# RWKV scan of a four-layer decoder step: the turned keys come out of the score products, and of the samples' state update only two row sums stay in the scan, the new state being formed during the output projection

## The reference, cut to what matters

```python
def step(S, inp):
    r_t, w_t, k_t, v_t, kk_t, a_t = inp
    sa = jnp.einsum('bhvk,bhk->bhv', S, -kk_t)
    S = (S * w_t[:, :, None, :] + sa[..., None] * (kk_t * a_t)[:, :, None, :]
         + v_t[..., None] * k_t[:, :, None, :])
    return S, jnp.einsum('bhvk,bhk->bhv', S, r_t)
...
y = y * lnx_w.astype(jnp.float32) + lnx_b.astype(jnp.float32)
bonus = jnp.sum(rh * kh * r_k.astype(jnp.float32), axis=-1, keepdims=True) * vh
out = ((y + bonus.reshape(B, T, D)).astype(x.dtype) * g) @ w_o
```

## Time and profile before

| what | value |
|---|---|
| median of 3 runs | 3062.38 us (3061.74 to 3062.84) |
| the profiled execution | 3060.58 us, its span 3058.5 us |
| busy: PE, DVE, ACT, POOL | 2906.5, 1550.4, 1050.5, 1327.6 us |
| the scan's loops, 927 to 1135 us | PE busy 187.25 of 208 us, DVE 160.74 |
| `out` of layer 1 | about 1204.9 to 1253.5 us |

### The profile page before, as it was taken

The page is one execution under the profiler, slowest core; times in us unless marked ns, Lnnn a source line. Parts: engine busy times, 40 slices in busy tenths (PEclk is TensorE's granted clock), DMA queues, the critical chain, the costliest instruction groups (busy, mean ns, idle before and its releaser), DMA issues.

```text
span 3058.5 us, 75513 instructions
## 1 busy us (share of the span) xinstructions
PE 2906.5 (95%) x30897; PEld 2751.0 (90%) x30897; DVE 1550.4 (51%) x2142; ACT 1050.5 (34%) x2027; POOL 1327.6 (43%) x949
## 2 busy tenths in 40 slices
PE   6999999998988989899999999989999999899998
PEld 6998999988977876899998799879999899799998
DVE  3435666127257775566612162466660345566612
ACT  4224333225443332433322443343332322433322
POOL 3443444442435554344444263534444344344443
PEclk8999999999999999999999899999999999899999
DMA  7544333543320003433354322443335543133332
GB/s 269 166 157 150 95 91 96 160 152 114 105 56 4 4 4 84 162 91 90 91 169 137 102 77 85 161 149 91 90 102 157 163 128 91 59 91 90 94 92 84
DMA packets 465628, 332.72 MB, mean 109 GB/s; under 512 B 19915, under 2 KB 435609, under 8 KB 465123
## 3 DMA queue, kind: packets, MB, share of 16 engines
q1 hardware_dynamic: 461400, 325.24, 34.4%
q10 hardware_dynamic: 4010, 4.22, 0.6%
HBM read 319.62 MB, written 10.20 MB: 108 GB/s over the span
## 4 chain that ended last, share of the span: by engine, by line
PE 56%; issue 5%; DVE 4%; POOL 3%; ACT 2%; DMA 1%; SPq 0%; POOLq 0%; DVEq 0%; ACTq 0%
PE banks L1616 33%; PE banks L1624 16%; POOL ct L894 2%; PE banks L2075 1%; DVE h L2557 1%; PE banks L1922 1%; PE banks L1577 1%; DVE proj L2501 1%; PE banks L1639 1%; PE banks L1710 0%; DMA s_state<-in_state_wkv_b_dram 0%; ACT conv L1065 0%; DVE proj_b L2501 0%; POOL mmt L885 0%; DMA w_raw<-in_ffn_w_up_dram 0%
## 5 line engine op out<-in xcount | busy, mean ns | idle before, releaser
L766 POOL TENSOR_TENSOR w_lo<-w_raw,w_hi 128x1024 fp32r<-128x1024 f32 x395 | 1005.2, 2545 | 1113.2 <-ACT w_hi L966 1093.2
L1616 PE MATMUL banks<-u_hi,w_hi 128*128 128x260 f32 x4064 | 835.5, 287 | 13.7 <-ACT w_hi L966 8.8
L1616 PE MATMUL banks<-u_lo,w_hi 128*128 128x260 f32 x4064 | 826.4, 285 | 0.0
L1616 PEld LDWEIGHTS banks<-u_hi,w_hi 128*128 128x128 f32 x4064 | 628.5, 190 | 27.1 <-issue 15.2
L1616 PEld LDWEIGHTS banks<-u_lo,w_hi 128*128 128x128 f32 x4064 | 631.1, 190 | 1.6
L966 ACT ACTIVATE w_hi<-w_raw 128x1024 fp32r<-128x1024 f32 x402 | 424.4, 1056 | 454.4 <-PE banks L1624 293.0
L1624 PE MATMUL banks<-u_hi,w_lo 128*128 128x260 f32 x4064 | 527.7, 282 | 0.0
L1624 PEld LDWEIGHTS banks<-u_hi,w_lo 128*128 128x128 f32 x4064 | 502.2, 187 | 1.5
L1616 PE MATMUL banks<-hid_hi,w_hi 128*128 128x260 f32 x1664 | 336.3, 283 | 0.0
L1616 PE MATMUL banks<-hid_lo,w_hi 128*128 128x260 f32 x1664 | 335.2, 283 | 0.0
L2991 DVE TENSOR_TENSOR csb<-proj 128x520 f32 (+1 forms) x42 | 29.9, 712 | 471.1 <-ACT proj L1033 471.1
(11 more groups left out here) (463 smaller groups left out, 3925.0 us busy)
## 6 DMA issues: line engine op xcount, KB each, us to landing
w_raw<-in_ffn_w_up_dram SPq DMA_DIRECT2D x176, 512.0 KB, 3.6
ada_raw<-in_ada_w_dram SPq DMA_DIRECT2D x96, 512.0 KB, 4.7
w_raw<-in_ffn_w_down_dram SPq DMA_DIRECT2D x64, 448.0 KB, 3.6
w_raw<-in_sconv_w_in_dram SPq DMA_DIRECT2D x48, 512.0 KB, 4.9
ada_ahead<-in_ada_w_dram SPq DMA_DIRECT2D x36, 512.0 KB, 7.3
ada_ahead_down<-in_ada_w_dram SPq DMA_DIRECT2D x36, 512.0 KB, 6.5
w_raw<-in_ffn_w_down_dram SPq DMA_DIRECT2D x32, 512.0 KB, 3.7
ada_pro<-in_ada_w_dram SPq DMA_DIRECT2D x6, 2048.0 KB, 20.5
```

Source lines behind the costliest of these rows:

```text
L766: pool.tensor_tensor(w_lo[:, s, :, :], w_raw[:, s, :, :], w_hi[:, s, :, :].bitcast(F32), ALU.subtract).then_inc(lo_done, 1)
L1616: pe.matmul(tile_ps[slot][half][0:width, 0:HALF], w_hi[:, s, k, 0:width], x[:, k0 + k, half * HALF:(half + 1) * HALF], start=start and k = ...
```

## The change

1. **Turned keys from the score products.** The moving operand `ZR` gets the identity as a third block of 64 columns, so the same product that makes the scores with B (or K) also leaves B (or K) turned. `turn_keys` is gone. `tok` exists twice, and ACT copies the turned keys per pair (`keys_out`, 128x128) behind the `t1` copies of levels 1 to 4, and the values before `uu`.
2. **Samples: two row sums in the scan.** `sample_rows` keeps four instructions per chunk (two products, two row sums, both from the old state). The output row follows from them and two dot products (`key_dots`).
3. **Samples: the new state in `out`.** `decay_state(c)`, five linked instructions of 128x512 for each eighth, 40 in all, runs on VectorE between the tile squares. SP's store of `s_state` moves behind the loads of `out` and ahead of those of `up`, and waits for `s_y_done` 2.

```diff
+                    def thirds(o, j):
+                        return o[:, HD:7 * HD].rearrange("p (n two t) -> p n two t", two=2, t=HD)[:, :, j, :]
...
-                        both(lambda rs: o[rs, HD:3 * HD], lambda rs: b["B"][rs, i, :], lambda rs: b["ZR"][rs, i, :])
+                        both(lambda rs: thirds(o, 0)[rs], lambda rs: b["B"][rs, i, :], lambda rs: b["ZR"][rs, i, :])
...
-                        both(lambda rs: o[rs, 3 * HD:5 * HD], lambda rs: b["K"][rs, i, :],
+                        both(lambda rs: thirds(o, 1)[rs], lambda rs: b["K"][rs, i, :],
...
                         if one_more:
                             pe.wait_ge(scores_masked, 4 * w + 8)
+                            pe.wait_ge(tok_ready, 6 * w + 10)
                             turn_values(cn, qn)
...
-                            pe.wait_ge(keys_built, w + 2)
-                            turn_keys(qn)
                             turn_inverse(w + 1, qn)
...
+                    def keys_out(w, q, i):
+                        act.wait_ge(scores_masked, 4 * w + i + 1)
+                        act.activation(tok[q][:, i, 0:2 * HD], bank[4 + (i + 1) % 4][:, SCW:SCW + 2 * HD], ACT.Copy)\
+                           .then_inc(tok_ready, 1)
...
+                            if one_more and lvl:
+                                keys_out(w + 1, 1 - q, lvl - 1)
...
+                        if one_more:
+                            values_out(w + 1, 1 - q)
                         act.wait_ge(u_mm, w + 1)
...
-                        if one_more:
-                            act.wait_ge(st_mm, w + 1)
-                            tokens_out(w + 1)
...
-                                sample_state(c, 5 * q)
-                            if lvl == 3 and q == 0:
-                                sample_state(c, 1)
-                        for j in range(2):
-                            sample_state(c, 4 * q + 2 + j)
+                                sample_rows(c, 2 * q)
+                        sample_rows(c, 2 * q + 1)
...
-                        sample_state(c, 4 * q + 4)
...
                     dve.wait_ge(sstate_loaded, 32)
-                    b0, s0, PER = base[0], step[0], 2 * 2 + 9
+                    for i, row in enumerate((4, 1)):
+                        link(dve.tensor_tensor(s_tmp[:, 0, :], s_vec[:, row, :], s_vec[:, 0, :], ALU.mult))
+                        link(dve.tensor_reduce(key_dots[:, i:i + 1], s_tmp[:, 0, :], AX.X, ALU.add))
+                    link(dve.tensor_tensor(s_vec[:, 0, :], s_vec[:, 0, :], s_vec[:, 5, :], ALU.mult))
+                    b0, s0, PER = base[0], step[0], 2 * 2 + 4
...
+                    def decay_state(c):
+
+                        vs, W = slice(KT * c, KT * (c + 1)), s_part[:, :, :]
+                        S = s_state[:, vs, :]
...
+                        link(dve.tensor_tensor(S, S, rows_of(5), ALU.mult))
+                        for values, keys in ((6, 4), (2, 1)):
+                            link(dve.tensor_tensor(W, cols_of(values), rows_of(keys), ALU.mult))
+                            link(dve.tensor_tensor(S, S, W, ALU.add))
...
+                            elif l % 3 == 1:
+                                for c in ((0,), (1, 2), (3,), (4, 5), (6,), (7,))[n]:
+                                    decay_state(c)
+                        if l % 3 == 1:
+                            dve.sem_inc(s_y_done, 1)
...
+                    if l % 3 == 1:
+                        sp.wait_ge(s_y_done, 2)
+                        for hh in range(2):
+                            sp.dma_start(O["wkv_b_sample"][0].rearrange("b (j a) v k -> a (b j) v k", a=2)[hh],
+                                         s_state[hh * HD:(hh + 1) * HD, :, :]).then_inc(s_state_out, 16)
```

More of the change, by code:

```diff
@@ L117, in trunk_kernel @@
         tail = sb("tail", [P, 2, 2 + NS])
+        key_dots = sb("key_dots", [P, 2])
         rows = sb("rows", [2 + NS, 2, P])
@@ L184, in trunk_kernel @@
             o = big_off + q * 8224
-            d = {"ZR": at(f"bd_ZR{q}", [P, 4, P], F32, o)}
-            for i, nm in enumerate(("B", "K", "Em")):
-                d[nm] = at(f"bd_{nm}{q}", [P, 4, HD], F32, o + 2048 + i * 1024)
+            d = {"ZR": at(f"bd_ZR{q}", [P, 4, 3 * HD], F32, o)}
+            for nm, at_ in (("B", (big_off + 6144, w_raw_at + 26624)[q]), ("K", o + 3072), ("Em", o + 4096)):
+                d[nm] = at(f"bd_{nm}{q}", [P, 4, HD], F32, at_)
             d["Ep"] = at(f"bd_Ep{q}", [P, 4, HD + 1], F32, o + 7 * 1024)
@@ L194, in trunk_kernel @@
         t1 = at("t1", [P, 4, HD], F32, w_raw_at + 13312)
-        tok = at("tok", [P, 4, 3 * HD], F32, w_raw_at + 14336)
+        tok = [at(f"tok{q}", [P, 4, 3 * HD], F32, w_raw_at + o) for q, o in enumerate((14336, 23552))]
         rhs_sb = at("rhs_sb", [P, 4, HD], F32, w_raw_at + 17408)
@@ L611, in _ @@
                 elif p["kind"] == "rwkv":
-                    sp.wait_ge(s_y_done, 1)
-                    for hh in range(2):
-                        sp.dma_start(O["wkv_b_sample"][0].rearrange("b (j a) v k -> a (b j) v k", a=2)[hh],
-                                     s_state[hh * HD:(hh + 1) * HD, :, :]).then_inc(s_state_out, 16)
                     sp.wait_ge(wkv_copied, 1)
@@ L742, in _ @@
                 select(sc_mask[rs, 0:HD], [[-1, HD]], 0, 1, ALU.is_gt)
-                for c0 in (HD, 3 * HD):
+                for c0 in (HD, 2 * HD):
                     select(sc_mask[rs, c0:c0 + HD], [[1, HD]], 0, -1, ALU.is_gt)
-                for c0 in (2 * HD, 4 * HD):
+                for c0 in (3 * HD, 4 * HD):
                     select(sc_mask[rs, c0:c0 + HD], [[1, HD]], 0, -1)
@@ L1372, in _, with values_out @@
                     ins.then_inc(sample_columns_ready, 1)
-                    def tokens_out(w):
-                        for i, (n, bk) in enumerate(((2, 4), (0, 1), (1, 3))):
-                            act.wait_ge(tok_done, 4 * w + i + 1)
-                            act.activation(tok[:, :, n * HD:(n + 1) * HD],
-                                           bank[bk][:, 0:4 * HD].rearrange("p (i t) -> p i t", i=4), ACT.Copy).then_inc(tok_ready, 1)
+                    def keys_out(w, q, i):
+                        act.wait_ge(scores_masked, 4 * w + i + 1)
+                        act.activation(tok[q][:, i, 0:2 * HD], bank[4 + (i + 1) % 4][:, SCW:SCW + 2 * HD], ACT.Copy)\
+                           .then_inc(tok_ready, 1)
+                    def values_out(w, q):
+                        act.wait_ge(tok_done, 2 * w + 1)
+                        act.activation(tok[q][:, :, 2 * HD:3 * HD], bank[4][:, 0:4 * HD].rearrange("p (i t) -> p i t", i=4),
+                                       ACT.Copy).then_inc(tok_ready, 1)
                     def turned_inverse(w, q):
-                        act.wait_ge(tok_done, 4 * w + 4)
+                        act.wait_ge(tok_done, 2 * w + 2)
                         act.activation(mmt[q][:, :, HD:2 * HD], bank[0][:, 4 * HD:8 * HD].rearrange("p (i t) -> p i t", i=4),
@@ L1416, in scan_step @@
                            .then_inc(y_ready, 1)
-                        if one_more:
-                            act.wait_ge(st_mm, w + 1)
-                            tokens_out(w + 1)
+                    for i in range(4):
+                        keys_out(0, 0, i)
+                    values_out(0, 0)
                     turned_inverse(0, 0)
-                    tokens_out(0)
                     act.wait_ge(srow_turned, 1)
@@ L1434, in _ @@
                     act.wait_ge(srow_turned, 2)
+                    act.activation(s_kept[:, :, :], s_vec[:, :, :], ACT.Copy)
                     act.activation(rw_y[:, :, TP:T], bank[6][:, 0:KT * NS].rearrange("p (b k) -> p k b", k=KT),
@@ L2097, in turn @@
                         mm.then_inc(tok_done, 1)
-                    def turn_keys(q):
-                        turn(lambda rs, i: bd[q]["B"][rs, i, :], 1)
-                        turn(lambda rs, i: bd[q]["K"][rs, i, :], 3)
                     def turn_inverse(w, q):
@@ L2525, in _ @@
                     xh, xl = (xb_hi, xb_lo) if p["full"] else (u_hi, u_lo)
-                    if l % 3 == 1 and mod is mod_f:
-                        dve.wait_ge(s_state_out, 32)
                     if l % 3 == 2 and mod is mod_f:
@@ L2891, in _ @@
                     dve.wait_ge(dve_step, base[0] + step[0])
+                    for i, row in enumerate((6, 2)):
+                        link(dve.scalar_tensor_tensor(s_vec[:, 7, :], s_vec[:, row, :], key_dots[:, i:i + 1], s_vec[:, 7, :],
+                                                      ALU.mult, ALU.add))
                     dve.sem_inc(s_y_done, 1)
@@ L3001, in sample_states @@
                         ins.then_inc(gs_ready, 1)
-                    if p["kind"] == "out" and l % 3 == 2:
+                    def decay_state(c):
+                        vs, W = slice(KT * c, KT * (c + 1)), s_part[:, :, :]
+                        S = s_state[:, vs, :]
```

(7 more changed lines are left out.)

52 lines of the change are left out of this document (20 added, 32 removed).

## The result

The changed kernel takes 3078.4 us (median of 5 runs, 3071.2 to 3081.2), before takes 3062.4 (5 runs). The ratio is 1.0047, 95% interval 1.0034 to 1.0060: slower by 14.4 us (10 to 18). The time alone lies nearer to the rival without queueing (3076) than to the forecast (3085), so it cannot tell the two apart; the profile does. The profiled execution has a span of 3076.6 us, 18.1 more than before's. I read it in the order of the prediction's steps.

A forecast was written before the change was run, and what follows sets the result against it. PE, busy 95% of the span, was taken as the bound. Scan -4.9, squares in `out` +24.5 and clock +3 gave +22.6 on 3060.58, so 3083.2; the median's 1.8 more made 3085 (62%), range 3069 to 3096.

The forecast's parts named there:

- the rival without queueing: End of `out`: the load for `up` does not queue behind the store; squares +16.8 us, time 3076; chance 13%.
- New states in `out`: VectorE in `out`: 28.8 us of state instructions, 8.9 for tiles, 12.5 lost beside `w_lo`; states formed at 1264.6.
- The store and the load behind it: End of `out`: ACT waits for `up`'s load behind the store, 12.5 us, middle of 9.1 and 15.9; squares +24.5.
- by bytes: Lower bound for `up`'s load behind the store: time goes by bytes, 9.1 us for 2 MB.
- VectorE's last sum is long done by then: End of `out`: VectorE's sum precedes the late squares, so the norm's chain moves by the whole +24.5 us.
- The clock: Norm behind `out`: small sums and spreads run at half speed for a while, +3 us, between 0 and 9.
- The scan: Scan: early tokens -6.8, turned keys -2.7, wider B product +3.3, small instructions +1.3; -4.9 us, bounds -14 and +2.
- that of the turned keys: End of a scan step: the `uu` copy covers most of 16 turning matmuls; 0.18 us saved, 15 times, -2.7 us.
- Tokens early and the wider products together: Scan steps: early token copies -6.8 us, wider B product +3.3 us, wider K product nothing.
- The rival that VectorE binds the scan: Scan: sample instructions that leave VectorE count in full, 34 us, time 3051; chance 4%.
- The one that VectorE and POOL hardly hold each other up: In `out`: states ready at 1252.1, squares +12.0 us, time 3070; chance 12%.
- that more is late than the squares: In `up`: the clock stays low or the second block waits too, time 3090 to 3098; chance 9%.

The follow-up runs named there:

- experiment 5: The run vectors_in_psum, on top of store_behind: the samples' row vectors copied into PSUM for 24 of 40 state instructions; 3060.0 us, ratio 0.9996 to before.
- loads_first: Changed kernel, SP still waiting for the state instructions, but issuing the first two loads of `up` before the store; 3061.3 us, ratio 1.0011 to before.
- half_store: Changed kernel with only one of the two halves of the samples' states stored; 3069.5 us, ratio 1.0037 to before.
- store_behind: Changed kernel with the store of the samples' states issued behind the first two loads of `up`; 3064.1 us, ratio 1.0014 to before.
- turns_again: Kernel with turned keys, early token copies and before's sample instructions and store, plus the 16 old turning matmuls, results unused; 3054.6 us, ratio 0.9979 to before.
- experiment 1: Two runs: changed kernel without new states, 3046.1 us, ratio 0.9956; turned keys and early tokens with before's sample instructions and store, 3044.8 us, ratio 0.9955.
- vectors_in_psum: store_behind with the samples' row vectors copied once into PSUM, so 24 of 40 state instructions read one operand there; 3060.0 us, ratio 0.9996 to before.
- twice_b: Kernel with turned keys, early token copies and before's sample instructions and store, plus the B product's third block run twice; 3049.5 us, ratio 0.9962 to before.

## Why the prediction was right, and which terms were off

The direction and the place held, and so did the range (3078.4 in 3069 to 3096, 6.6 below the forecast). But the change that was forecast is 22.6 us and the measured one 14.4, and that gap is one sum, the scan's, which came out at the very edge of the -14 to +2 that it was given. The number was held by the width of the range there, not by the working. Step by step:

- **New states in `out`**: predicted 50.2 us from the first square to the last state, measured 50.35, with the six stretches of 2.08 lost. Right, and by the predicted cause: the six rows of 2.8 us beside `w_lo`, and experiment 5 for what makes them.
- **The store and the load behind it**: 12.5 us was a middle between "by bytes" and "behind the landing"; it measured 14.1. The step named the queue, and this part of it fell: another queue took 1 us off, half of the bytes 4.6. The rival without queueing said +16.8 us at the squares, which is what loads_first measured (+16.3): its price was right, but not for this kernel, where the store goes first. That the middle came near was luck: the bound "by bytes" had the price of the store right (4.6 us for 1 MB in half_store, 4.55 by layer 2), but not the load's own landing behind it, 4.3 us in loads_first; 9.2 and 4.3 make 13.5.
- **"VectorE's last sum is long done by then"**: right here, 13.5 us ahead of the squares. But the squares wait for that sum by themselves (15 us behind the old distance in store_behind). So moving the store could give back only 11 of the 26 us.
- **The clock**: +3 predicted, 2.3 to 2.8 from the squares to the first `gate` in all runs with states in `out`, 1.7 of it in the 32 products above. Right.
- **The scan**: -4.9 predicted, -13.5 measured by the ratio (loops -9.3 in the profiled execution of the changed kernel, -12.4 in the mean of the eight with its scan, against the one execution of before). This is the mis-sized sum. The term that failed is that of the turned keys: "the `uu` copy covers them. I take 0.18". It measured 0.63 a step, 9.5 us instead of 2.7, in the trace, and 7.3 by the times. I had read one quiet step; in before's mean the y products start 0.40 us late, not 0.21, and the matmuls delay PE's stream at later places as well. Tokens early and the wider products together were put at -3.5; turns_again against before gives -2.4 in the trace (15.17 against 15.01, 15 times), which is within the spread of one scan, and -6.4 by the times (-8.9 to -3.7). So part of the missing 8.6 us may lie there, and the two are not told apart. K at nothing and the samples' leaving at nothing were right as far as can be seen. The small instructions cost 1.9, not 1.3. The loops and this start give -10.5; the 3 us from there to -13.5 are within the interval, and I did not find their place.
- The sum of the profiled execution: -6.0 at the first square (which holds 2.25 us that its scan began late), +26.2, +2.3, -4.4 given back: +18.1. By the ratios it is the forecast's +22.6, less 8.6 for the scan, plus 1.7 for `out`, less 0.7 for the clock: 15.0, against 14.4 measured (0.0047 x 3062). The 4.4 given back have no place in that sum; they are not shown to be more than chance of one execution.

The rival that VectorE binds the scan is refuted by experiment 1. The one that VectorE and POOL hardly hold each other up is refuted by the six rows of 2.8 us, the one that the load does not queue by ACT's 30.28 us and the 14.1. For the last one, that more is late than the squares, `up` began 22.5 us late and no later, and the end came 18.1 late.

## What to carry to other kernels

Work that is taken out of a stage where its engine has slack gains nothing there. Put between the tiles of the next one it fills that engine's pauses first and moves the end by what is left: here some 41 us of work moved the last square by 15 (store_behind), and by 26 with the store that had to wait for it. Find out by a run with each half alone which half of a change pays, and keep that. A matmul that stands beside a copy is not free because the copy's consumer starts on time; where the engine is the bound, count what it issues over a whole stage. Before a difference of two profiled executions is called an effect, see how far executions of one and the same stage lie apart; here it was 5 us of 214. A store that must come late is issued behind the small loads that the next stage opens with, and changing its queue didn't replace that here.

## What the runs showed of the hardware

- A load of 512 KB that came right behind a 2 MB store (its own issue 0.4 and 3.8 us behind the store's) was there 13.1 us behind the store's issue with the two on different queues, and 14.0 us with both on SP's; behind 1 MB of store it was there 9.4 us behind the store's issue; issued first, it was there within 3.8 us of its own issue. Whether the size of the store's pieces does that was not tried.
- VectorE's 128x512 instruction with one operand in PSUM took 0.69 us beside a running GpSimd `w_lo` (vectors_in_psum), the one with both in SBUF up to 2.78 (the changed kernel).
- Stretches in which PE's weight loads wait for nothing that the profile shows came to 13.2 to 20.4 us in the loops of the ten kernels without the extra matmuls, and to 22.0, 23.1 and 24.1 in turns_again, twice_b and before. In the eight executions of one and the same scan they mostly rise with its length. I had counted such matmuls by their issue time alone. What PE waits for there stays open.
